# Part order of split fp32 products, quarter-wise loads of an expert pair, and the loads and norms at a kernel's start

## The reference

```
def first_block(x, ...):
    h = _rmsnorm(x, g_pre_mix[i]);  proj = h @ w_in[i]
    ...                                             # two mixers
    merged = gm[:, :, 0] * (o_nsa @ w_br_nsa[i]) + gm[:, :, 1] * (o_mla @ w_br_mla[i])
    x = x + _rmsnorm(merged @ w_o[i], g_post_mix[i])
    h = _rmsnorm(x, g_pre_ffn[i]);  u = _causal_dwconv(h @ w_up[i], w_conv[i], b_conv[i])
    x = x + _rmsnorm((jax.nn.gelu(a) * v) @ w_down[i], g_post_ffn[i])
    gate = sigmoid(x @ w_ple_gate[i]);  x = x + _rmsnorm(e * gate, g_ple[i])
def second_block(x, ...):
    x = mixer_sublayer(x, ...)                      # begins with rmsnorm and h @ w_in_2
    x = x + hierarchical_moe(rmsnorm(x, norm2_g[i]), ..., w_gate[i], w_up[i], w_down[i])
```

## Time and profile before

| | us |
|---|---|
| median of 3 runs | 1580.74 |
| lowest and highest | 1578.43, 1581.37 |
| the profiled execution's own time | 1582.54 |
| its span, first to last instruction | 1580.8 |
| PE busy in the span | 1497.3 |
| mean granted TensorE clock | 0.985 of full |

### The profile page before, as it was taken

The page is one execution under the profiler, slowest core; times in us unless marked ns, Lnnn a source line. Parts: engine busy times, 40 slices in busy tenths (PEclk is TensorE's granted clock), DMA queues, the critical chain, the costliest instruction groups (busy, mean ns, idle before and its releaser), DMA issues.

```text
span 1580.8 us, 18974 instructions
## 1 busy us (share of the span) xinstructions
PE 1497.3 (95%) x7434; PEld 1005.5 (64%) x7435; DVE 646.5 (41%) x1083; ACT 513.2 (32%) x914; POOL 473.0 (30%) x251
## 2 busy tenths in 40 slices
PE   7999999999999999999999999998799998999996
PEld 6985667888788888878867777467344443433343
DVE  3155665223643333331144677673433232332234
ACT  5236666222543333321146432524111111111012
POOL 4440125444434444444424254532100000000000
PEclk9999999999999999999999999999799999999999
DMA  7333001222232332223213322257799999999995
GB/s 305 106 108 92 2 1 41 94 94 94 84 117 94 100 101 94 94 94 105 95 67 121 100 80 80 107 213 299 295 396 429 430 431 430 428 429 428 425 423 224
DMA packets 48568, 306.15 MB, mean 194 GB/s; under 512 B 6704, under 2 KB 6832, under 8 KB 35168
## 3 DMA queue, kind: packets, MB, share of 16 engines
q1 hardware_dynamic: 43552, 290.56, 47.6%
q0 software_dynamic: 4352, 12.27, 2.1%
q10 hardware_dynamic: 576, 2.10, 0.4%
HBM read 302.87 MB, written 4.19 MB: 194 GB/s over the span
## 4 chain that ended last, share of the span: by engine, by line
PE 75%; DMA 11%; DVE 5%; ACT 3%; POOL 2%; issue 2%; SPq 1%; DVEq 0%; ACTq 0%; POOLq 0%
PE banks L411 28%; PE banks L1130 11%; PE banks L441 10%; DMA ring<-experts 10%; PE banks L1161 4%; PE banks L2260 2%; PE banks L421 2%; PE banks L971 2%; PE banks L1170 2%; PE banks L2189 1%; POOL arena_r L374 1%; PE banks L829 1%; PE banks L830 1%; PE banks L2205 1%; DMA arena<-arena 1%
## 5 line engine op out<-in xcount | busy, mean ns | idle before, releaser
L374 POOL TENSOR_TENSOR arena_r<-ring,arena_r 128x1024 fp32r<-128x1024 f32 x143 | 351.7, 2464 | 434.1 <-ACT arena_r L359 414.8
L411 PE MATMUL banks<-hT_r,arena_r 128*128 128x512 f32 x1216 | 388.2, 390 | 3.9 <-POOL arena_r L374 2.4
L359 ACT ACTIVATE arena_r<-ring 128x1024 fp32r<-128x1024 f32 x143 | 150.6, 1058 | 457.8 <-PE banks L411 300.5
L411 PE MATMUL banks<-arena_r 128*128 128x512 f32 x800 | 291.6, 389 | 0.0
L411 PEld LDWEIGHTS banks<-hT_r,arena_r 128*128 128x128 f32 x1216 | 228.3, 188 | 56.9 <-issue 7.4
L1130 PE MATMUL banks<-ring,arena 128*64 128x512 f32 x720 | 222.3, 604 | 16.2 <-DMA ring<-experts 15.9
L441 PE MATMUL banks<-arena_r 128*128 128x512 f32 x784 | 184.1, 389 | 2.5 <-POOL arena_r L374 1.9
L411 PEld LDWEIGHTS banks<-arena_r 128*128 128x128 f32 x800 | 150.2, 188 | 30.9 <-issue 0.2
L441 PEld LDWEIGHTS banks<-arena_r 128*128 128x128 f32 x784 | 147.0, 188 | 34.2 <-POOL arena_r L374 3.8
L1130 PEld LDWEIGHTS banks<-ring,arena 128*64 128x64 f32 x720 | 71.8, 139 | 150.6 <-issue 150.6
L1745 DVE TENSOR_TENSOR resid<-resid,banks 128x1024 f32<-128x1024 f32 x63 | 74.0, 1217 | 130.3 <-PE banks L1170 130.3
(11 more groups left out here) (443 smaller groups left out, 1875.3 us busy)
## 6 DMA issues: line engine op xcount, KB each, us to landing
ring<-stream SPq DMA_DIRECT2D x162, 512.0 KB, 3.6
arena<-experts SPq DMA_DIRECT2D x40, 2048.0 KB, 16.9
ring<-experts SPq DMA_DIRECT2D x37, 2048.0 KB, 16.7
ring<-experts SPq DMA_DIRECT2D x12, 1024.0 KB, 14.3
arena<-experts SPq DMA_DIRECT2D x12, 1024.0 KB, 16.1
arena<-experts SPq DMA_DIRECT2D x9, 512.0 KB
ring<-experts SPq DMA_DIRECT2D x8, 512.0 KB, 7.4
resid<-x ACTq DMA_DIRECT2D x4, 512.0 KB, 5.7
```

The lines of the kernel that those rows point to most:

```text
L359: nc.scalar.activation(parts(name, m)[:, 0, :], tile(tile_n), ACT.Copy).then_inc(S["w_high"], 1)
L374: nc.gpsimd.tensor_tensor(w[:, 1, :], tile(tile_n), plain(w[:, 0, :]), ALU.subtract).then_inc(S["w_low"], 1)
L411: last = nc.tensor.matmul(pb[:, bank, :], w[:, a, k * P:(k + 1) * P], b[:, k, :], start=(k == 0 and part == 0), stop=(k == ND - 1 and part ...
```

## The change

1. **Low part last.** In `split_features`, for every tile but the first of a stage, PE waits for `w_high`, does the 16 products with the high part, waits for `w_low`, and does the 8 products with the low part. The shared merge tiles but number 0 do the same, and tile 0 waits for the mixers' low parts one k at a time. In `split_tokens`, k = 1 and the middle ks do the high part, then the low part (`staged`).
2. **First gate tile.** The first feature tile of the merge does the high-part products of k = 0 to 3 before it waits for `w_low`, and then goes on k by k.
3. **Up chunks in quarters.** Pair 0's up product raises `gate_part` too, and SP loads pair 1's up chunks quarter by quarter. Chunk 0 of pair 3 is issued in the midst of pair 2's loads, ahead of its up chunks.
4. **Start.** The identity is loaded first, on SP's queue. All ring loads wait for `x_in1` alone, the columns follow two ring tiles on SP's queue, and POOL's tables wait for the columns. ACT takes a root of a constant before x arrives. The first weight tile's low part is formed by DVE, the second tile's high part by POOL.
5. **Last norm tile by halves.** In n1, n2 and n3 the last tile is scaled in two halves, and PE starts its transposes after the first (`norm_half`). In n2 the sum of squares of the last tile is shared: ACT does the first half, DVE the second, and the root adds them.

```diff
@@ split_features
-            pe.wait_ge(S["w_low"], SPLIT_TILES.index(SPLIT[name][0] + m) + 1)
+            n = SPLIT_TILES.index(SPLIT[name][0] + m) + 1
+            if m != first:
+                pe.wait_ge(S["w_high"], n)
+                for k in range(ND):
+                    for part, b in enumerate((high, low)):
+                        nc.tensor.matmul(pb[:, bank, :], w[:, 0, k * P:(k + 1) * P], b[:, k, :], start=(k == 0 and part == 0), stop=False)
+                pe.wait_ge(S["w_low"], n)
+                for k in range(ND):
+                    last = nc.tensor.matmul(pb[:, bank, :], w[:, 1, k * P:(k + 1) * P], high[:, k, :], start=False, stop=(k == ND - 1))
...
+            ahead = 3 if name == "merge" else 0
...
+                if k == ahead:
+                    pe.wait_ge(S["w_low"], n)
@@ split_tokens
+            def staged(k, tiles):
...
+                pe.wait_ge(S["w_high"], n)
...
+                if high is None:
+                    pe.wait_ge(S["rows_low"], rows)
+                for i in tiles:
+                    one(k, i, ((0, 0), (1, 0)))
+                pe.wait_ge(S["w_low"], n)
+                for i in tiles:
+                    last = one(k, i, ((0, 1), ))
@@ expert_stream
-            for q, (signal, count) in enumerate((("gate_part", 1), ("gate_part", 2), ("gate_part", 3), ("ex_gate", 1))):
...
+            for base, whole in ((0, "ex_gate"), (2, "ex_up")):
+                for q in range(4):
+                    part = slice(1024 * q, 1024 * q + 1024)
+                    sp.wait_ge(*((S["gate_part"], 3 * (base // 2) + q + 1) if q < 3 else (S[whole], 1)))
+                    for c in range(base, base + 2):
+                        sp.dma_start(chunk(c)[:, part], EX[6 + c, :, part]).then_inc(chunk_in[c], 16)
             for b in range(1, N_PAIR - HALVED):
-                for c in range(2 if b == 1 else 0, 6):
+                for c in range(4 if b == 1 else 1 if b == SPARE[0] + 1 else 0, 6):
+                    if b == SPARE[0] and c == 2:
+                        sp.wait_ge(done[0], b)
+                        sp.dma_start(chunk(0), EX[6 * (b + 1), :, :]).then_inc(chunk_in[0], 16)
@@ SyncE
+            sp.dma_start(cst[:, 0:P + 1], csts[:, 0:P + 1]).then_inc(S["x_in0"], 16)
+            sp.wait_ge(S["x_in1"], 16)
             for s in range(RING):
-                if s < 2:
-
-                    sp.wait_ge(S[f"x_in{1 + 2 * s}"], 16)
+                if s == 2:
+                    sp.dma_start(colt[:, :], cols).then_inc(S["cols_in"], 16)
@@ GpSimd
+            nc.gpsimd.tensor_copy(second_weight[:, 0, :], tile(W_PROJ_FM + 1)).then_inc(S["w_high"], 1)
+            pool.wait_ge(S["w_low"], 1)
+            low_pool(pool, "proj", 1, 2)
+            pool.wait_ge(S["cols_in"], 16)
@@ ScalarE
+            act.wait_ge(S["dve_chain"], 1)
+            nc.scalar.activation(st[:, 449:450], st[:, 448:449], ACT.Sqrt)
...
+                    if i == NT - 1:
+                        first_half_square(act, n, X[:, i, :])
+                        shared_root(act, n)
@@ VectorE
+            dve.wait_ge(S["w_high"], 1)
+            nc.vector.tensor_tensor(first_weight[:, 1, :], tile(W_PROJ_FM), plain(first_weight[:, 0, :]), ALU.subtract)\
+                .then_inc(S["w_low"], 1)
...
+                if i == NT - 1:
+                    dve.wait_ge(S["post_x"], NT)
+                    second_half_square(dve, X[:, i, :], xn2)
```

More of the change, by code:

```diff
@@ L164 @@
     + [(n, i) for n in ("n4", "n5") for i in range(NT)]
+SHARED = ("n2",)
 SPLIT_TURNS = ("n1", "n2", "x2", "n3")
@@ L428, in split_tokens, with one @@
             base, K, _ = SPLIT[name]
-            def one(k, i):
+            def one(k, i, terms=((0, 0), (0, 1), (1, 0))):
                 w = parts(name, k)
@@ L438, in one @@
                     u = [high[:, f, i * P:(i + 1) * P], low[:, f, i * P:(i + 1) * P]]
-                for part, (row, v) in enumerate(((0, 0), (0, 1), (1, 0))):
+                for row, v in terms:
                     for h in range(2):
                         last = nc.tensor.matmul(pb[:, 2 * i + h, :], u[row], w[:, v, h * 512:(h + 1) * 512],
-                                                start=(k == 0 and part == 0), stop=(k == K - 1 and part == 2))
+                                                start=(k == 0 and row + v == 0), stop=(k == K - 1 and row == 1))
+                return last
+            def staged(k, tiles):
+                n = SPLIT_TILES.index(base + k) + 1
+                rows = SPLIT_ROWS.index((name, k)) + 1 if high is None else 0
+                pe.wait_ge(S["w_high"], n)
+                if name == "w_o" and k >= 2:
+                    pe.wait_ge(S["h_high"], ND + k - 1)
+                    for i in tiles:
+                        one(k, i, ((0, 0), ))
+                    pe.wait_ge(S["w_low"], n)
+                    for i in tiles:
+                        one(k, i, ((0, 1), ))
+                    pe.wait_ge(S["rows_low"], rows)
+                    for i in tiles:
+                        last = one(k, i, ((1, 0), ))
+                    return last
+                if high is None:
+                    pe.wait_ge(S["rows_low"], rows)
+                for i in tiles:
+                    one(k, i, ((0, 0), (1, 0)))
+                pe.wait_ge(S["w_low"], n)
+                for i in tiles:
+                    last = one(k, i, ((0, 1), ))
                 return last
@@ L453, in split_tokens @@
                 for k in range(2):
+                    if q == 0 and k == 1:
+                        last = staged(k, pairs[q])
+                        continue
                     if q == 0:
@@ L460, in split_tokens @@
             for k in range(2, K - tail):
-                have(k)
-                for i in range(NT):
-                    last = one(k, i)
-                last.then_inc(S["w_used"], 1)
+                staged(k, range(NT)).then_inc(S["w_used"], 1)
             if tail > 2:
@@ L1108, in both_in @@
                     left = 1 if v in SPARE and (not isinstance(b, int) or b > SPARE[v]) else 0
-                    if v < 2 and (not isinstance(b, int) or b >= 1):
+                    if v < 4 and (not isinstance(b, int) or b >= 1):
                         left -= 3
@@ L2016, in tr_pe @@
             for a, b in order:
-                if ready is not None and b == 0:
+                if ready is not None and a == A - 1 and b == 0:
+                    pe.wait_ge(S["norm_half"], before // A + 1)
+                elif ready is not None and b == (B // 2 if a == A - 1 else 0):
                     pe.wait_ge(ready, before + a + 1)
@@ L2521, in L @@
                 link(dve, chain, ins)
+            L(nc.vector.memset(st[:, 448:449], 1.0))
             for i in range(NT):
                 norm_scale(dve, chain, "n1", i)
+            first_weight = parts("proj", 0)
+            dve.wait_ge(S["w_high"], 1)
+            nc.vector.tensor_tensor(first_weight[:, 1, :], tile(W_PROJ_FM), plain(first_weight[:, 0, :]), ALU.subtract)\
+                .then_inc(S["w_low"], 1)
             dve.wait_ge(S["cols_in"], 16)
```

96 lines of the change are left out of this document (64 added, 32 removed).

## The result

The changed kernel takes 1568.93 us (median of 4 runs, 1568.52 to 1572.45) against 1580.74: a ratio of 0.993, 95% interval 0.9918 to 0.9942, or 11.8 us less. That is 1.1 us off the forecast and inside the range. Several of its terms are off, though, and they cancel.

A forecast was written before the change was run, and what follows sets the result against it. PE bounds the kernel nearly everywhere ahead of the experts, the DMA stream from 1178 to 1483 us. Terms 2.3 + 2.0 + 1.9 + 1.0 + 1.5 + 2.0 = 10.7 us give a median of 1570.0, range 1566 to 1576.

The forecast's parts named there:

- start: Start of the kernel: identity with x, early root and DVE's weight part bring PE's first product 2.3 us sooner (0.4 to 2.8).
- merge: Merge's first tiles: PE no longer waits for all low parts or for POOL; 2.0 us won (1.2 to 2.4).
- w_o and down, second tiles: Second tiles of w_o and down: waits for POOL of 0.94 and 0.96 us go, 1.9 us won.
- norms n2, n3: Last tile of n2 and n3: halved scaling and n2's shared square win 1.0 us together (0.5 to 1.2).
- in2: in2: high-part products cover POOL's late low parts, 1.5 us won (1.0 to 1.65).
- added waits: One or two more waits inside accumulations in 112 tiles: cost 0 to 1.8 us, taken as 0.
- stream: Experts' loads: early chunk 0 of pair 3 and up chunks in quarters win 2.0 us together (0.8 to 2.8).
- clock: Rival: the lower clock after the experts' last chunk wait vanishes with it, gain up to 14 us, 1566 to 1568; chance 0.08.
- the step that named DVE's weight part as deciding: Start: the first weight tile's low part on DVE, over at 12.8 us, decides when DVE begins the activation's low parts.
- The 0.5 us for POOL's copy: Start: DVE loses 0.5 us to POOL's copy of the second weight tile, released by the same signal; between nothing and 2.40.
- the split between chunk and quarters: Experts' stream: chunk 0 of pair 3 gives 1.7 us, the quarters of the up chunks 0.3.
- partly given back: Rival: gains ahead of the experts partly return to DVE or POOL; 4 to 7 us left, about 1575; chance 0.17.

The follow-up runs named there:

- the second trace of before: The kernel before, unchanged, run once more for a second profile: 1580.43 us, ratio 0.9999.
- the second comparison: The changed kernel once more, unchanged, with a second profile, against the kernel before on the same chip: 1569.66 us, ratio 0.9927.

## Why the prediction was right, and where it was not

| term | forecast | measured in the traces |
|---|---|---|
| start | 2.3 | 1.6 |
| merge | 2.0 | 1.6 |
| w_o and down, second tiles | 1.9 | 2.5 |
| norms n2, n3 | 1.0 | 0 |
| in2 | 1.5 | 1.9 |
| added waits | 0 | 0 |
| stream | 2.0 | 2 to 3 |
| mixers | not in it | 0.35 |
| clock | 0 | +3.4, -1.7, +1.7, +1.1 in the first profile; varies |
| sum | 10.7 | 10.0 to 11.0 without the clock |

The medians differ by 11.8 us, with an interval of 9.2 to 13.0. The sum fits, but that the median came within 1.1 us of the forecast is in part luck: the start, the merge and the norms, 2.1 us too high together, are made good by w_o, down, in2, the mixers and perhaps the stream.

- **Start: the step that named DVE's weight part as deciding failed.** The last root ended at 10.67 for 10.4, near the forecast but by another way. The forecast read the row at 4.77 as ACT waiting for the identity; it is a table load of 1.28 us in front of the first square. In the second trace of before ACT waited for the identity for only 0.19 us behind that load. So the dummy root took two table loads off ACT's way behind x, and the first square went from 6.14 to 5.10, 1.04 us and not 1.3, where the identity now holds it. What the identity's new place gives by itself was not tried. The columns, which the change put behind x and two ring tiles, landed at 13.25. The forecast took their 0.36 MB off x's path and didn't ask who waits for them; and it set the transposed banks ready at 12.6, where they were at 12.9. The 0.5 us for POOL's copy did not fall on DVE: DVE came first, and POOL's copy took 1.42 us for 1.04 (its time in the kernel with the columns first) instead. The Trainium skill (SBUF — State Buffer, "SBUF: two separate sides") has the two exclude each other for a whole instruction. This trace agrees: DVE's subtraction ran from 11.70 to 12.92, its usual 1.22 us, and POOL's copy, begun at 12.39, ended at 13.81.
- **Merge:** right for the shared tiles (2.3 us at the first gate tile), with 1.6 of 2.0 for the stretch; wrong in what it gave to the delayed low part of that tile, worth 0.3 us. DVE's step late was forecast at up to 0.6 us and came as 0.48.
- **w_o, down, in2:** the right places, each 0.3 to 0.4 us too small, in part since the terms were taken from idle times that begin at a modelled end.
- **Norms: failed.** Shortening the last tile's chain wins only if PE waits for it. In n2 the transposes before it kept PE busy at the lower clock in 13 of 14 traces, and in n3 they ran on into those of the last tile as well.
- **Stream:** right in place and mechanism, and in the split between chunk and quarters.
- **Clock:** the rival was given 0.08 as a gain of its own. The forecast argued that the clock stood at 1.00 through the experts' waits. That holds for the first trace alone; each of the other 13 has 6.8 to 10.2 us at the lower level among those waits, where the stream sets the pace and no cost shows. Behind the last wait the clock fell in 2 of 14 traces: the first one of before, not its second, and the kernel with the old stream. So it does not hang on the change. In the first profile this lapse did vanish, one at 112 us as well, and one appeared at 1049. From the two profiles alone one would read a gain of 14.1 us. The medians say 11.8, and those of the second comparison 10.0 (its ratio of 0.9927, 11.5).
- **The gains did not collide:** "partly given back" came true only as the 0.48 us at the merge.

What the prediction asked for is met at the first product of the experts (1108.75 for about 1110; 10.5 us earlier for 8 to 9, of which the clock gave 1.7 or more), in up's spacing and in the waits for chunks (13.0 for 14). The merge's feature tiles came 7.9 us earlier for 4 to 5, 3.4 of it from the clock. The first product of proj missed, 14.96 for 14.2.

## What to carry to other kernels

Where a second operand comes late only at a few places, doing the products that don't need it first wins exactly the waits that the trace shows there and nothing elsewhere, at no cost for the waits that it adds. Before you shorten a chain ahead of an engine, look whether that engine has a pause there at all, at either level of its clock. When transfers are reordered, ask of each one moved back who waits for it. When an engine starts late, read what it does in that time: a table load is work, and not a wait. And before a change is read from two profiles, profile one kernel twice.

## What was not expected of the hardware

- TensorE's clock falls to 1.2 GHz at places that repeat only in part: at n2, behind a pause of 2.5 us, in 13 of 14 traces; near 112 us in 6, and there for 3.4 or 6.8 us. Two executions of one kernel differ by 3.4 us in proj to merge for that (233.91 and 237.30). The spans of the changed kernel's repeat went from 1565.1 us at a mean clock of 0.986 to 1570.1 at 0.981.
- DVE's subtraction of 128 x 1024 with both inputs in SBUF took 1.22 us, less than twice the 128 x 512 one (0.68).
- POOL's copy of 128 x 1024 took 1.04 us alone and 1.42 beside DVE's subtraction.
